# Identity products on TensorE in front of its waits, in a two-block transformer kernel on one core

## The chip, the cores and the metric

The program runs on one core of one Trainium2 chip. The metric is the device time of one execution in microseconds (us). Before the change three executions took 2232.43, 2234.43 and 2234.75 us, median 2234.43.

## What is computed

The reference applies two models of two layers each to 256 tokens of width 1024, in float32, one after the other.

```python
x = first_block(x, ...)     # per layer: mixer_block, layer_norm, then swiglu (layer 0) or moe_ffn (layer 1), layer_norm
return second_block(x, ...) # per layer: modulated rms_norm, attention, modulated rms_norm, gated feed-forward
```

The mixer of the first block projects the tokens with one wide matrix into four branches (windowed attention, an RWKV recurrence, a forgetting attention called fox, and a top-k attention called dsa) and four gates, and joins them. The mixture of experts routes each token to two of eight experts:

```python
logits = (x @ router_w).astype(jnp.float32) + router_b
top_val, top_idx = lax.top_k(logits, TOP_K)
weights = jax.nn.softmax(top_val, axis=-1)
...
y = y + combine[..., e:e + 1].astype(x.dtype) * swiglu(x, w1[e], w3[e], w2[e])
```

The second block adds `g * f(rms_norm(x) * (1 + sc) + sh)` twice per layer, where g, sc and sh are rows made from a conditioning vector.

## The kernel before, in words

Each engine has its own hand-written program; they meet through semaphores. TensorE's program (`pe`, from line 1150) sets the order of the work. The tokens lie as two tiles (t = 0, 1) of 128 rows by 1024 columns; `turn` (line 1172) transposes one tile with eight transposes against the identity matrix `ident`, ScalarE copies the result from PSUM to `xT`, and products against weights follow: `channel_tile` (line 1255) and `token_tile` (line 1262), eight 128-row steps each. Weights come in units of 1 MB (in the experts smaller ones) that SyncE's queue loads into a ring of slots as they come free. One ordinary float32 product call shows as two MATMUL records in the trace, one transpose as one. Independent projections, handed out by `fill`, stand between dependent steps so that TensorE has work while the other engines compute. Where none is left, TensorE waits on a semaphore.

The waits that the change touches, in order of the program:

- **Start** (lines 1696 to 1710): TensorE waits for `ident` from GpSimd, then for the first tokens, and turns them.
- **Mixing** (`tanh`, line 1722): after the projections of the RWKV branch TensorE waits for ScalarE's tanh of the low-rank row (line 855), then makes `w_up`, `a_up` (lines 1725, 1729) and `g_up` (line 1734), in both layers.
- **Attention entry** (line 1875, layer 0): TensorE waits for `pick`, VectorE's scores of the top-k branch (line 2492), before the first attention products (`scores`, line 1522). The fox heads there use products with only four active rows (lines 1526 and 1527).
- **Routing** (lines 1900 to 1911 and `experts`, line 1326): for each tile TensorE turns it and multiplies by the router (line 1904); VectorE finds the two experts (`assigned`); TensorE counts ranks (lines 1330 to 1334); VectorE derives the number of rounds (`rounds`, line 2109) and the gather matrices (line 2127); TensorE loads the number of rounds into a register and gathers the tokens (line 1361).
- **Second block's entry** (`spread`, line 1212): in layer 0 TensorE waits for VectorE's variance of the first tile, then spreads two rows of the modulation over all partitions (line 1220) with four calls of 512 columns. Then the first tile is scaled and turned by products against a diagonal matrix (`turn_scaled`, line 1182), which waits for VectorE's line 2553. In layer 1 `spread(1)` stands after the first two projections, and the third (`project`) waits for VectorE to free its PSUM bank (line 2300).

```python
pe.wait_ge(*ready("dve", "rounds"))
n_rounds = pe.value_load(rounds_i[0:1, 0:1], min_val=1, max_val=3)
...
with S.turns(pe, n_rounds):
    for k in range(KT):
        gather_tokens(0, k)
```

Of the kernel before, what the change touches and what calls it, by code (L numbers as in the profile page):

```python
# [14 lines left out]
P = 128  # L15
# [62 lines left out]
class Signals:  # L78
# [26 lines left out]
    def ready(self, kind, *key, back=0):  # L105
        value, looped = self.known.value[(kind, key)] if self.known else (1, False)
        if looped:
            step = self.known.per_turn[kind]
            return self.sem(kind), self.turn * step + (value + self.credit(kind) - back * step)
        return self.sem(kind), value  # L110
# [19 lines left out]
def build(nc, a, out, known):  # L130
    with ExitStack() as ctx:
# [3 lines left out]
        def sb(name, shape, dt=F32):  # L135
            return ctx.enter_context(nc.sbuf_tensor(name, shape, dt))
# [15 lines left out]
        ident = sb("ident", [P, P])  # L152
# [17 lines left out]
        psum = ctx.enter_context(nc.psum_tensor("psum", [P, 8, 512], F32))  # L170
# [980 lines left out]
        def _(pe):  # L1151
# [3 lines left out]
            def job(ins, *key):  # L1155
                ins.then_inc(*made("pe_job", *key))
# [7 lines left out]
            def used(*key):  # L1164
                S.also("pe_job", "unit", *key)

            def turn(src, tag, t, made_by=None):

                if made_by is not None:
                    pe.wait_ge(*ready("dve", *made_by, t))  # L1170
                for k in range(KT):
                    ins = pe.transpose(psum[:, 2 * t + k // 4, (k % 4) * P:(k % 4) * P + P],
                                       src[:, t, k * P:k * P + P], ident[:])
                job(ins, "xt", *tag, t)
# [11 lines left out]
            def modulated(which, l, t):  # L1186
                pe.wait_ge(*ready("dve", "modulated", which, l, t))
                pe.wait_ge(*ready("act", "modulated", which, l, t))
# [17 lines left out]
            def turn_mod(l, bank):  # L1206

                pe.wait_ge(*ready("mod_turned", l))
                ins = pe.transpose(psum[:, bank, 0:48], mod_turned[0:48, :], ident[0:48, 0:48])
                job(ins, "mod_columns", l)  # L1210

            def spread(l):

                pe.wait_ge(*ready("pool", "g_diag", l))
                if l == 0:
                    pe.wait_ge(*ready("dve", "var", "ln2", 1, 0))
                    pe.wait_ge(*ready("act", "warm", "ln2", 1))
                for i in range(2):
                    for h in range(2):
                        ins = pe.matmul(psum[:, 4 + 2 * i + h, :], ones[:],  # L1220
                                        g_diag[:, i, 4 * h:4 * h + 4].rearrange("p a b -> p (a b)"),
                                        start=True, stop=True)
                    job(ins, "spread", l, i)
# [102 lines left out]
            def experts():  # L1326

                pe.wait_ge(*ready("pool", "numbers"))
                pe.wait_ge(*ready("dve", "assigned"))
                pe.matmul(psum[:, 5, 0:8], before[:], assigned[:, 0, :], start=True, stop=True)  # L1330
                pe.matmul(psum[:, 5, 8:16], ones[:], assigned[:, 0, :], start=True, stop=False)
# [2 lines left out]
                job(pe.matmul(psum[:, 5, 16:24], ones[:], assigned[:, 1, :], start=False, stop=True), "ranks")  # L1334
                pe.wait_ge(*ready("dve", "rounds"))
                n_rounds = pe.value_load(rounds_i[0:1, 0:1], min_val=1, max_val=3)

                def xjob(ins, *key):
                    ins.then_inc(*made("x_pe", *key))
# [345 lines left out]
            for l in range(DEPTH):  # L1685
                if l == 0:
                    pe.wait_ge(*ready("pool", "ident"))
                first = []
                for t in range(NT):
                    if l == 0:  # L1690
# [29 lines left out]
                else:  # L1720
                    turn_mod(0, PAR_BANK)
                fill(l, G[0][l] - 1, (6,))
                pe.wait_ge(*ready("act", "tanh", l))
                for ct in range(2):
                    ins = pe.matmul(psum[:, 0, ct * 256:ct * 256 + 256], lora[0:64, l, 0, ct * P:ct * P + P],
# [44 lines left out]
                for c in range(NC):  # L1770

                    b = (0, 1, 4, 5)[c]
                    for h in range(4):
# [4 lines left out]
                                  start=True, stop=True)  # L1778
# [7 lines left out]
                for lv in range(1, 6):  # L1786
# [11 lines left out]
                    for g in range(2):  # L1798
                        pe.wait_ge(*ready("act", "U", l, lv, g))
                        for m in range(4 * g, 4 * g + 4):  # L1800
                            for odd in range(2):
                                o = (m % 4) * CH
                                pe.matmul(psum[hb(odd), 4 * g + 1, o:o + CH], TT[hb(odd), m, :], U[hb(odd), m, :],
                                          start=True, stop=True)
# [57 lines left out]
                for qt in range(NT):  # L1862
                    nk = P * (qt + 1)
                    for h2 in range(2):
                        for h in range(2):
                            ins = pe.matmul(psum[:, 4 + 2 * qt + h, h2 * 256:h2 * 256 + nk],
                                            dsa_qi[hb(h), h2, qt * P:qt * P + P], dsa_ki[hb(h), 0:nk],
                                            start=True, stop=True)
                    job(ins, "idx", l, qt)
                fill(l, in_attention(l), (0, 1))  # L1870
                for b in (0, 1):
                    if b in fill_in:
                        pe.wait_ge(*ready("act", "filled", l, fill_in[b]))

                pe.wait_ge(*ready("dve", "pick", l, NT - 1))
                attention(l)
                barrier()
# [4 lines left out]
                for c in range(KT):  # L1882
                    if c >= 2:
                        pe.wait_ge(*ready("dve", "prod", l, c - 2))
                    for b in range(4):
                        rows_of = (range(0, 4), range(4, 6), range(6, 8), range(8, 10))[b]
                        dst = psum[:, 4 + 2 * (c % 2) + b // 2, (b % 2) * 256:(b % 2) * 256 + 256]
                        for k in rows_of:
                            ins = pe.matmul(dst, (wb_first[:, k] if k < 5 else wb_last[:, k - 5])[:, c * P:c * P + P], oT[:, k, :],  # L1889
                                            start=(k == rows_of[0]), stop=(k == rows_of[-1]))  # L1890
# [3 lines left out]
                def normalised(t):  # L1894
                    turn(x, ("f1", l), t, ("ln", "ln1", l))
                    pe.wait_ge(*ready("act", "xt", "f1", l, t))

                if l == 0:
                    dense(("ffn1", 0), normalised)
                else:  # L1900
                    for t in range(NT):
                        normalised(t)
                        for k in range(KT):
                            ins = pe.matmul(psum[:, 4, t * 8:t * 8 + 8], xT[:, k, t * P:t * P + P], router[:, k, :],
                                            start=(k == 0), stop=(k == KT - 1))
                    job(ins, "router")
                    pe.wait_ge(*ready("dve", "router_logits"))
                    experts()

            for l in range(DEPTH):  # L1910

                if l == 0:
                    spread(0)
                else:
                    turn_mod(1, 3)
                first = []
                for t in range(NT):
                    turn_scaled("mix", l, t)
                    modulated("mix", l, t)
                    for n in range(2):  # L1920
                        if t == 0:
                            first.append(unit("in2", l, ORDER2[n]))
                        ins = token_tile(psum[:, n, t * 256:t * 256 + 256], first[n], 0, 256, t)
                        if t == 1:
                            job(ins, "in2", l, ORDER2[n])
                            used("in2", l, ORDER2[n])
                if l == 1:
                    spread(1)
                del turned_last[:]
                project(l, 2)  # L1930
                turn_heads(l, 0)
                project(l, 3)
                turn_heads(l, 1)
                project(l, 4)
                turn_heads(l, 3)
                scores2(l, 0)
                project(l, 5)
                turn_heads(l, 4)
                turn_probs2(l, 0)
                scores2(l, 1)  # L1940
                project(l, 6)
                weigh2(l, 0)
                turn_probs2(l, 1)
                scores2(l, 2)
                project(l, 7)
                turn_heads(l, 6)
                turn_outs(l, 0)
                weigh2(l, 1)
                turn_probs2(l, 2)
                scores2(l, 3)  # L1950
                project(l, 8)
                turn_heads(l, 7)
                turn_outs(l, 1)
                weigh2(l, 2)
                turn_probs2(l, 3)
                project(l, 9)
                turn_outs(l, 2)
                weigh2(l, 3)
                scores2(l, 4)
                project(l, 10)  # L1960
                turn_heads(l, 9)
                turn_probs2(l, 4)
                turn_outs(l, 3)
                scores2(l, 5)
                project(l, 11)
                turn_heads(l, 10)
                weigh2(l, 4)
                turn_probs2(l, 5)
                join(l, 0, 0)
                join(l, 0, 1)  # L1970
                scores2(l, 6)
                turn_outs(l, 4)
                weigh2(l, 5)
                join(l, 0, 2)
                join(l, 0, 3)
                scores2(l, 7)
                turn_probs2(l, 6)
                turn_outs(l, 5)
                join(l, 0, 4)
                join(l, 0, 5)  # L1980
                join(l, 1, 0)
                turn_probs2(l, 7)
                weigh2(l, 6)
                join(l, 1, 1)
                join(l, 1, 2)
                turn_outs(l, 6)
                weigh2(l, 7)
                join(l, 1, 3)
                join(l, 0, 6)
                turn_outs(l, 7)  # L1990
                join(l, 1, 4)
                join(l, 0, 7)
                join(l, 1, 5)
                join(l, 1, 6)
                join(l, 1, 7)

                def gated(t):
                    turn_scaled("ffn", l, t)
                    modulated("ffn", l, t)

                dense(("ffn2", l), gated)
# [699 lines left out]
```

## Time and profile before

| | us |
|---|---|
| median of three executions | 2234.43 |
| the profiled execution's own time | 2232.85 |
| its span, first to last instruction | 2231.1 |
| TensorE matmul busy in the span | 2116.5 (95%) |
| VectorE busy | 658.6 (30%) |
| ScalarE busy | 363.8 (16%) |
| mean granted TensorE clock | 0.981 of full |

### The profile page before, as it was taken

How to read it: one execution, taken by the hardware profiler on the slowest of the kernel's cores; microseconds unless marked ns; L12 is line 12 of the kernel's file. 1: busy time of each engine (PE TensorE's matmuls, PEld its weight loads, DVE VectorE, ACT ScalarE, POOL GpSimd, SP SyncE). 2: the span in 40 equal slices, each digit the busy share in tenths (PEclk: the TensorE clock that was granted, in tenths of full speed). 3: DMA queues.
4: the chain of work that ended last, by engine and by line, in shares of the span. 5: the costliest groups of instructions: out<-in, count | busy, mean ns of one | idle time of the engine just before them, and what ended most of it. 6: DMA issues, size and time to landing. Idle time of an engine off the chain costs nothing.

```text
span 2231.1 us, 33975 instructions
## 1 busy us (share of the span) xinstructions
PE 2116.5 (95%) x14688; PEld 1525.7 (68%) x14688; DVE 658.6 (30%) x1635; ACT 363.8 (16%) x861; POOL 83.7 (4%) x180
## 2 busy tenths in 40 slices
PE   8998999999989999998999999899999998999998
PEld 7786776777678877855643553487677757867776
DVE  1415424333334154242010000244433333440001
ACT  1312230000013122300010000133200012430000
POOL 3000000000000000020000000000000020000000
PEclk9999999999999998998999999999999999999999
DMA  8333234688563342337999999942579763224442
GB/s 254 114 96 123 95 123 151 210 274 285 173 193 105 93 139 82 123 97 248 348 313 371 345 323 364 298 133 95 177 232 306 255 183 113 96 95 151 134 149 94
DMA packets 333817, 421.23 MB, mean 189 GB/s; under 512 B 27222, under 2 KB 282148, under 8 KB 333668
## 3 DMA queue, kind: packets, MB, share of 16 engines
q1 hardware_dynamic: 312464, 352.96, 49.1%
q0 software_dynamic: 13408, 50.66, 6.8%
q10 hardware_dynamic: 7796, 15.43, 2.0%
q8 instruction: 116, 1.90, 0.4%
q14 instruction: 33, 0.27, 0.0%
HBM read 417.90 MB, written 1.05 MB: 188 GB/s over the span
## 4 chain that ended last, share of the span: by engine, by line
PE 87%; DVE 4%; ACT 3%; issue 2%; DMA 2%; ACTq 1%; POOL 0%; DVEq 0%; POOLq 0%
PE psum L1255 31%; PE psum L1372 10%; PE psum L1262 9%; PE psum L1273 9%; PE psum L1432 5%; PE psum L1889 3%; PE psum L1502 2%; PE psum L1673 2%; PE psum L1291 2%; PE psum L1361 1%; PE psum L1700 1%; PE psum L1445 1%; DVE arena L2061 1%; ACTq L635 1%; DMA arena<-in_w_mod 1%
## 5 line engine op out<-in xcount | busy, mean ns | idle before, releaser
L1255 PE MATMUL psum<-xT,ring 128*128 128x256 f32 x3520 | 786.4, 384 | 3.9 <-ACT small L758 2.1
L1255 PEld LDWEIGHTS psum<-xT,ring 128*128 128x128 f32 x3520 | 672.5, 192 | 118.9 <-issue 20.5
L1273 PE MATMUL psum<-ring,arena 128*128 128x512 f32 x528 | 232.8, 594 | 0.0
L1262 PE MATMUL psum<-ring,xT 128*128 128x256 f32 (+2 forms) x960 | 205.5, 373 | 11.8 <-DVE arena L2300 4.4
L1262 PEld LDWEIGHTS psum<-ring,xT 128*128 128x128 f32 x960 | 174.4, 194 | 39.9 <-DVE arena L2300 5.7
L1273 PEld LDWEIGHTS psum<-ring,arena 128*128 128x128 f32 x528 | 100.3, 191 | 114.9 <-issue 112.5
L2072 DVE TENSOR_TENSOR arena<-arena,psum 128x512 f32<-128x512 f32 x33 | 22.7, 687 | 407.4 <-PE psum L1255 235.0
L2061 DVE SCALAR_TENSOR_TENSOR arena<-arena,cond 128x256 f32<-128x256 f32 x336 | 135.0, 478 | 0.0
L1372 PE MATMUL psum<-ring,arena 128*32 128x256 f32 x2304 | 126.9, 379 | 0.7 <-DVE arena L2144 0.7
L667 ACT ACTIVATE arena<-psum 128x512 f32<-128x512 f32 x33 | 19.7, 597 | 578.2 <-PE psum L1255 571.9
L1372 PEld LDWEIGHTS psum<-ring,arena 128*32 128x32 f32 x2304 | 74.6, 110 | 51.3 <-issue 3.4
L561 POOL DMA_DIRECT2D arena<-in_w_mod x48 | 42.5, 891 | 1331.7 <-PE psum L1673 605.3
L2152 DVE TENSOR_TENSOR arena<-arena,psum 128x768 f32<-128x768 f32 (+1 forms) x12 | 10.6, 887 | 218.1 <-ACT arena L689 218.1
L1889 PE MATMUL psum<-oT,arena 128*128 128x256 f32 x320 | 69.6, 380 | 4.2 <-DMA arena<-in_w_branch 4.2
L1889 PEld LDWEIGHTS psum<-oT,arena 128*128 128x128 f32 x320 | 60.6, 190 | 13.2 <-DMA arena<-in_w_branch 5.0
L1372 PE MATMUL psum<-arena 128*32 128x256 f32 x1152 | 64.9, 380 | 0.0
L1432 PE MATMUL psum<-ring,arena 128*32 128x512 f32 x576 | 64.2, 594 | 0.0
L1673 PE MATMUL psum<-ring,oT 128*128 128x512 f32 x128 | 56.9, 592 | 0.0
L1502 PE MATMUL psum<-ring,arena 128*128 128x512 f32 x128 | 55.3, 592 | 0.0
L1372 PEld LDWEIGHTS psum<-arena 128*32 128x32 f32 x1152 | 37.0, 110 | 24.6 <-issue 1.0
L1291 PE MATMUL psum<-xT,ring 128*128 128x128 f32 x384 | 44.4, 276 | 9.3 <-ACT xT L968 7.0
L744 ACT ACTIVATE arena<-psum,par 128x256 f32<-128x256 f32 x64 | 26.9, 471 | 161.1 <-PE psum L1255 161.1
(392 smaller groups left out, 1865.5 us busy)
## 6 DMA issues: line engine op xcount, KB each, us to landing
ring<-in_w_in SPq DMA_DIRECT2D x80, 1024.0 KB, 5.4
ring<-in_exp_w SPq DMA_DIRECT2D x312, 256.0 KB, 6.0
arena<-in_w_mod POOLq DMA_DIRECT2D x48, 1024.0 KB, 10.1
ring<-in_ffn_w SPq DMA_DIRECT2D x33, 1024.0 KB, 6.1
arena<-in_exp_w SPq DMA_DIRECT2D x120, 256.0 KB, 6.8
ring<-in_w_gate SPq DMA_DIRECT2D x22, 1024.0 KB, 7.7
ring<-in_w_up SPq DMA_DIRECT2D x22, 1024.0 KB, 10.1
ring<-in_w_down SPq DMA_DIRECT2D x22, 1024.0 KB, 5.1
```

Of the source, the lines that this page charges most:

```text
L561: pool.dma_start(modw[:, j % 3, :].rearrange("p (k c) -> p k c", k=KT), w_mod[:, :, j * UNIT:(j + 1) * UNIT]).then_inc(*made("modw%d" % (j ...
L744: step(act.activation(zb[:, b, c, :], bank[:, i * 256:i * 256 + 256], ACT.Identity, bias=prm(l, "gate_b", b * KT + c)), "filled", l, j)
L1255: ins = pe.matmul(dst, w[:, k * 256 + c0:k * 256 + c0 + m], act_t[:, k, :], start=(k == 0), stop=(k == KT - 1))
L1262: ins = pe.matmul(dst, act_t[:, k, t * P:t * P + P], w[:, k * 256 + c0:k * 256 + c0 + n], start=(k == 0), stop=(k == KT - 1))
L1273: ins = pe.matmul(psum[:, 4 + 2 * t + h, :], gT[:, s % 3, f * 256 + t * P:f * 256 + t * P + P], w2[:, f * D + h * 512:f * D + h * 512 + 51 ...
L1291: ins = pe.matmul(psum[:, i, f * 256 + t * P:f * 256 + t * P + P], wt[i][:, k * 256 + f * P:k * 256 + f * P + P], xT[:, k, t * P:t * P + P ...
L1372: ins = pe.matmul(psum[GRP * (g % 4):GRP * (g % 4) + GRP, o[0] + g // 4, o[1]:o[1] + n], xgT[:, k, GRP * g:GRP * g + GRP], slot[:, w0:w0 + n],
L1432: ins = pe.matmul(psum[GRP * (g % 4):GRP * (g % 4) + GRP, 3 * d + g // 4, :], hT[:, j, GRP * g:GRP * g + GRP], slot[:, w0:w0 + 512], start ...
L1502: ins = pe.matmul(psum[:, 2 * t + h, :], mergedT[:, k, t * P:t * P + P], ws[k2][:, i * D + h * 512:i * D + h * 512 + 512], start=(k == 0), ...
L1673: ins = pe.matmul(psum[:, 4 * t + h, :], oT8[:, k, t * P:t * P + P], w[:, (k % 2) * D + h * 512:(k % 2) * D + h * 512 + 512], start=(k == ...
L1889: ins = pe.matmul(dst, (wb_first[:, k] if k < 5 else wb_last[:, k - 5])[:, c * P:c * P + P], oT[:, k, :], start=(k == rows_of[0]), stop=(k ...
L2061: free(dve.scalar_tensor_tensor(out=pmod[:, i, :], in0=w, scalar=cond[:, k:k + 1], in1=pmod[:, i, :], op0=ALU.mult, op1=ALU.add), "mod", l, i)
```

## The change

A helper `keep_clock(bank, n)` issues n products of the identity matrix with itself, 128 by 128 each, into a PSUM bank that nothing reads at that point. It is called nine times, 81 products in all, 162 MATMUL records. No other instruction is added, removed or moved on any engine. In TensorE's program each call stands behind whatever it had to wait for before that place, and ahead of the wait named here.

| place | products | ahead of the wait for |
|---|---|---|
| start | 6 | first tokens |
| mixing, layer 0 | 4 | tanh |
| mixing, layer 1 | 10 | tanh |
| attention entry, layer 0 | 10 | pick (behind the wait for the last projection's copy) |
| routing, between the tiles | 5 | second tile normalised |
| routing, after the logits | 8 | assigned |
| routing, after the register load | 18 | gather matrices |
| second block, layer 0 | 6 | variance of the first tile |
| second block, layer 1, after spread(1) | 14 | bank of the third projection |

```diff
+            def keep_clock(bank, n):
+
+                for _ in range(n):
+                    pe.matmul(psum[:, bank, 0:P], ident[:], ident[:], start=True, stop=True)
...
                 pe.wait_ge(*ready("pool", "g_diag", l))
                 if l == 0:
+                    keep_clock(3, 6)
                     pe.wait_ge(*ready("dve", "var", "ln2", 1, 0))
...
                 pe.wait_ge(*ready("pool", "numbers"))
+                keep_clock(0, 8)
                 pe.wait_ge(*ready("dve", "assigned"))
...
                 n_rounds = pe.value_load(rounds_i[0:1, 0:1], min_val=1, max_val=3)
+                keep_clock(0, 18)
...
                 if l == 0:
                     pe.wait_ge(*ready("pool", "ident"))
+                    keep_clock(7, 6)
...
                 fill(l, G[0][l] - 1, (6,))
+                keep_clock(7, (4, 10)[l])
                 pe.wait_ge(*ready("act", "tanh", l))
...
+                if l == 0:
+                    keep_clock(3, 10)
                 pe.wait_ge(*ready("dve", "pick", l, NT - 1))
                 attention(l)
...
                     for t in range(NT):
+                        if t == 1:
+                            keep_clock(7, 5)
                         normalised(t)
...
                 if l == 1:
                     spread(1)
+                    keep_clock(3, 14)
```

## Rows read from the trace of the kernel before

**Rows 1.** The page: busy time, granted clock in 40 slices, and the chain.

```profile
PE 2116.5 (95%) x14688; PEld 1525.7 (68%) x14688; DVE 658.6 (30%) x1635; ACT 363.8 (16%) x861; POOL 83.7 (4%) x180
...
PEclk9999999999999998998999999999999999999999
...
PE 87%; DVE 4%; ACT 3%; issue 2%; DMA 2%; ACTq 1%; POOL 0%; DVEq 0%; POOLq 0%
```

**Rows 2.** Stretches: length, busy of PE, PEld, DVE, ACT, POOL, granted clock, DMA.

```profile
202.80:206.20 3.40, 0.52 (x7) 0.55 (x8) 3.15 (x8) 1.27 (x1) 0.00 (x0) 1.00 0.96 295
206.20:209.60 3.40, 3.40 (x11) 2.25 (x9) 2.67 (x7) 0.00 (x0) 0.00 (x0) 0.50 0.09 27
243.70:247.10 3.40, 3.40 (x17) 2.07 (x15) 0.00 (x0) 0.00 (x0) 0.00 (x0) 1.00 0.31 106
247.10:250.60 3.50, 3.50 (x9) 2.83 (x9) 3.19 (x8) 1.03 (x5) 0.00 (x0) 0.51 0.00 0
1015.20:1022.00 6.80, 6.19 (x10) 3.46 (x11) 1.11 (x2) 0.48 (x1) 0.00 (x0) 0.50 1.02 340
1022.00:1028.80 6.80, 6.80 (x22) 4.02 (x22) 1.11 (x2) 1.44 (x3) 0.00 (x0) 1.00 1.07 341
```

**Rows 3.** Timeline, one of the fox products in the first of the stretches at 243.7.

```profile
246.04 0.69 PE L1526 MATMUL psum<-arena,ident 4*128 4x256 f32 x2
```

**Rows 4.** Timeline, attention entry: start, us, engine, line, idle before and releaser.

```profile
205.68 1.22 PE L1522 MATMUL psum<-arena 64*128 64x128 f32 x8 [3.78 <-DVE arena L2492]
```

**Rows 5.** Timeline, mixing in layer 0 (first two) and layer 1.

```profile
65.49 0.48 PE L1725 MATMUL psum<-arena,lora 64*128 64x256 f32 x1 [0.99 <-ACT arena L855]
...
68.18 2.11 PE L1255 MATMUL psum<-xT,ring 128*128 128x256 f32 x9
...
670.32 0.74 PE L1725 MATMUL psum<-arena,lora 64*128 64x256 f32 x1 [3.79 <-ACT arena L855]
...
673.99 2.32 PE L1255 MATMUL psum<-xT,ring 128*128 128x256 f32 x10
```

**Rows 6.** Timeline, routing.

```profile
992.53 1.95 PE L1904 MATMUL psum<-router,xT 128*128 128x8 f32 x16 [1.16 <-ACT xT L658]
996.87 1.97 PE L1172 MATMUL psum<-ident,x 128*128 128x128 f32 x8 [2.39 <-DVE x L2038]
1000.00 3.58 PE L1904 MATMUL psum<-router,xT 128*128 128x8 f32 x16 [1.16 <-ACT xT L658]
...
1006.71 0.56 PE L1330 MATMUL psum<-arena 128*128 128x8 f32 x2 [3.13 <-DVE arena L2100]
...
1011.46 0.88 SPq L465 DMA_DIRECT2D oT<-in_exp_w  x2
...
1015.81 13.63 PE L1361 MATMUL psum<-arena,x 128*128 128x384 f32 x32 [6.83 <-DVE arena L2127]
```

**Rows 7.** Timeline, entry of the second block, layer 0.

```profile
1427.42 5.37 PE L1220 MATMUL psum<-arena,ones 128*128 128x512 f32 x8 [2.58 <-issue]
...
1432.43 0.29 DVE L2553 TENSOR_SCALAR arena<-ident,small 128x128 f32<-128x128 f32 x1
...
1432.77 2.05 PE L1182 MATMUL psum<-arena,x 128*128 128x128 f32 x16
```

**Rows 8.** Timeline, second block, layer 1.

```profile
1843.93 7.14 PE L1262 MATMUL psum<-ring,xT 128*128 128x256 f32 x32 [1.75 <-DVE arena L2583]
...
1850.91 3.60 PE L1220 MATMUL psum<-arena,ones 128*128 128x512 f32 x8
...
1858.92 10.20 PE L1262 MATMUL psum<-ring,xT 128*128 128x256 f32 x32 [4.41 <-DVE arena L2300]
```

**Rows 9.** Timeline, start of the program.

```profile
1.24 0.29 POOL L511 TENSOR_SCALAR_AFFINE_SELECT ident<-ident 128x128 f32<-128x128 f32 x1 [0.24 <-POOL ident L510]
...
4.81 1.94 PE L1172 MATMUL psum<-ident,x 128*128 128x128 f32 x8 [4.81 <-POOL tri L507]
7.91 9.17 PE L1700 MATMUL psum<-xT,ring 128*128 128x128 f32 x64 [1.16 <-ACT xT L658]
```

## The prediction

> **What bounds the kernel now.** I read the page first. TensorE is busy for 95% of the span and holds 87% of the chain that ended last [rows 1]. The reader should see two consequences: a microsecond less on TensorE is nearly a microsecond less of time, and products added between its waits cost nothing only as long as they end before the wait does. Then the clock row: all 9s but for two 8s [rows 1]; the mean is 0.981. Cutting the span into stretches shows where the halves lie. At the attention entry TensorE is nearly idle from 202.8 to 206.2, at clock 1.00; then it is busy throughout from 206.2 to 209.6, at 0.50 [rows 2]. The clock falls behind the idle time, and it is the work after the wait that pays. The same pattern stands behind the waits for tanh in layer 1, for the second tile in routing, for the gather, and at both entries of the second block. The idle times ahead of the fallen clock are 3.78 us at the attention entry [rows 4], 3.79 for tanh in layer 1 [rows 5], 2.39 and then 6.83 in routing [rows 6], 2.58 in the second block's layer 0 [rows 7] and 4.41 in layer 1 [rows 8]. The 0.99 us in front of tanh in layer 0 brought no fall [rows 5].
>
> Not every fall follows idleness: from 243.7 to 247.1 TensorE is busy throughout, with fox products of four rows among its work, and the clock is halved from 247.1 [rows 2, 3]. The change leaves those places alone.
>
> **What an added product costs.** A call gives two records of 128 columns. At full clock 16 ordinary records of that shape take 2.05 us [rows 7], and 16 of the router 1.95 [rows 6]: 0.12 to 0.13 us each, I take 0.12. At half clock the router's 16 take 3.58 [rows 6] and eight transposes 1.97: 0.22 to 0.25, I take 0.23. A call is thus 0.24 us warm and 0.46 cold.
>
> For bf16 the Trainium skill (TensorE: Matmul & The Clock Gate, "Wait — 56ns, not 53.3ns?") has 56 ns for 128 columns warm and 107 cold; by its figures all fillers below would cost half and none would overrun its wait, which would add the 2.5 us of overrun below to the gain. The float32 rows here show twice those figures, and the sum goes by the rows.
>
> **Place by place.**
>
> *Start.* `ident` is there at 1.53, the first product starts at 4.81 [rows 9]: 3.3 us, into which 12 cold records (2.8 us) fit. The row of granted clock is not recorded here, but the durations tell: eight transposes take 1.94 us where 0.12 each would be 1.0 [rows 9]. The next 64 records take 9.17 us; at 0.12 they would take 7.7. So at most 0.9 + 1.5 = 2.4 us is to be had, if the clock rises before 4.8; at the least nothing. I take the middle, 1.2.
>
> *Mixing, layer 0.* Eight records, 1.0 us, in 0.99 us of idle time [rows 5]. The clock stays up anyway: 0, at worst 0.1 lost. *Layer 1.* Twenty records, 2.4 us, in 3.79: 1.4 us of idleness are left. From L1725 to the projection behind it takes 2.69 us in layer 0 (65.49 to 68.18) and 3.67 in layer 1 at half clock (670.32 to 673.99) [rows 5]: **1.0**.
>
> *Attention entry.* Behind the copy that it waits for (about 202.8) 20 records end at 205.2, ahead of 205.68 [rows 4]. The stretch 206.2 to 209.6 is then at full clock: half of 3.4 is 1.7 [rows 2], less a little for waits, **1.6**. TensorE has projections queued behind, so this stays.
>
> *Routing.* Gains: ten of the 32 gather records run cold, 6.19 us where at full clock 22 take 6.80 (0.31 each): +3.2 [rows 2]. The second tile's router products 3.58 against 1.95: +1.6, of which I count half, since those eight-column products do little to hold a clock that the five calls before them raised [rows 6]. Costs: the eight calls start near 1003.9, when the logits are read. Cold they take 3.7 us, to 1007.6, and the rank counts behind them started at 1006.71 [rows 6]: 0.9 late cold, nothing warm; I take 0.5. The eighteen calls start once the register is loaded; SyncE, which loads the same number, issues at 1011.46 [rows 6], so 4.3 us are left to 1015.81. Thirty-six records take 4.3 us warm and 8.3 cold: 0 to 4.0 late. Half and half they are 2.0 late, which I take, since TensorE has been idle or nearly so for long before them and starts them cold. Sum 3.2 + 0.8 - 0.5 - 2.0 = **1.5**. The bounds are +5.6 (3.2 + 1.6 and 0.8 for the cold rank counts) and -4.9.
>
> *Second block, layer 0.* Twelve records, 1.4 us, fit in 2.58. The spread products would take 3.60 [rows 8] instead of 5.37 [rows 7], 1.8 less, but the next product starts at 1432.77, right behind VectorE's diagonal matrix, ready at 1432.72 [rows 7]. That becomes the wait: **0**. The dip behind 1438.4 follows other waits and stays.
>
> *Second block, layer 1.* Twenty-eight records, 3.4 us, in 4.41. The 32 projection records take 10.20 us instead of 7.14 [rows 8]: up to 3.0. This half clock lasts twice as long as the others; with one of the usual length it would be 1.6. I take the mean, **2.3**.
>
> **Sum:** 1.2 + 1.0 + 1.6 + 1.5 + 0 + 2.3 = 7.6 us, with bounds of the terms from about +13 to -1. Against the profiled 2232.85 that is 2225.3; against the median, which is 1.58 higher, **2226.8 us**. What also moves: all later work starts earlier, and the falls after fox products will land otherwise; about 2 us either way.
>
> **The rivals.**
>
> *The clock falls just the same (slower).* If multiplying the identity does not count as work for the clock, the gains are nil and the fillers still stand in the way: in routing 0.9 + 4.0 us at half clock, elsewhere they fit. 2234.4 + 4.9 = 2239.3. For it speaks that busy TensorE with four-row products did not hold the clock [rows 2, 3]; against it, that the filler has 128 active rows like the products that do. It decides if the stretch behind the attention entry and that behind spread(1) still read 0.50. The Trainium skill (TensorE: Matmul & The Clock Gate, "Part 4: PE-mode transpose") has that transposes do not count as busy for the clock in the same way. By that rule, were it to reach identity products, this rival would be the outcome; here the filler is an ordinary product, and no row shows identity products alone. Chance 0.08.
>
> *Held, but eaten (same).* The clock is held, but routing overruns fully while its gather still gains (3.2 - 4.9 = -1.7), the start gives nothing, and layer 1's spread gives 1.6: 1.0 + 1.6 - 1.7 + 1.6 = 2.5 us, 2231.9; or VectorE becomes the wait behind mixing and attention and takes 1 to 2 us back. For it: VectorE's 3.15 of 3.40 us at the attention entry [rows 2]. Chance 0.22.
>
> *The forecast,* 2222 to 2230, with its centre at 2226.8. Chance 0.70.
>
> **How the numbers follow.** A measurement of this kernel can tell about 0.2%, 4.5 us, from no change: faster means under 2230.0, slower over 2238.9. So faster 0.70, same 0.22, slower 0.08. The range runs from 2222 (start and routing both near their best) to 2233, which takes in the second rival and leaves out the first and the extremes.
>
> **What would show it.** In the changed profile the stretches behind tanh in layer 1, behind the attention entry, behind spread in layer 0 and behind spread(1) read 1.00; the 32 records after spread(1) take about 7.1 us; L1725 to the next projection 2.7; the gather's 32 records near 10.5 instead of 13.6. The gather starts later after the rank counts than the 9.1 us of before (1006.71 to 1015.81) if I am right on the overrun. The mean clock rises from 0.981 to about 0.99. A gather that starts on VectorE's release, with no filler ahead of it, would show the routing cost too high, and half clock behind any of the four fillers would show the mechanism wrong there.

## The result, and the profile after

| | before | changed |
|---|---|---|
| median, us | 2239.20 | 2227.93 |
| lowest to highest | 2230.62 to 2245.74 | 2218.88 to 2232.29 |
| executions | 16 | 16 |
| profiled execution, us | 2232.85 | 2223.20 |
| mean granted clock in it | 0.981 | 0.986 |

The ratio is 0.995, with a 95% interval from 0.9936 to 0.9963: 11.2 us faster, between 8.3 and 14.3. The median before is 4.8 us above that of the three executions shown first, which lie in the lower half of its range. So the predicted time, 2226.8, is met within 1.1 us and its range (2222 to 2233) holds it, but the predicted gain of 7.6 us is below the measured interval. Two errors of the forecast met: it started too low and took off too little.

The page of the changed kernel answers to [rows 1]:

```profile
PE 2127.5 (96%) x14850; PEld 1542.0 (69%) x14850; DVE 658.9 (30%) x1635; ACT 363.3 (16%) x861; POOL 83.3 (4%) x180
...
PEclk9999899999999999989999999999999999999999
```

TensorE has 162 records more and is busy for 11.0 us more in a span that is 9.6 us shorter. Four of the nine calls stand here, in the timeline of the changed kernel (start, us, engine, line, operation, count, idle before and releaser); line 1170 is the filler:

```profile
203.07 2.50 PE L1170 MATMUL psum<-ident 128*128 128x128 f32 x20 [0.93 <-ACT arena L744]
205.83 0.93 PE L1530 MATMUL psum<-arena 64*128 64x128 f32 x8 [0.26 <-DVE arena L2507]
...
664.27 2.44 PE L1170 MATMUL psum<-ident 128*128 128x128 f32 x20
668.21 0.48 PE L1735 MATMUL psum<-arena,lora 64*128 64x256 f32 x1 [1.50 <-ACT arena L855]
...
1416.48 1.50 PE L1170 MATMUL psum<-ident 128*128 128x128 f32 x12
1419.17 3.70 PE L1226 MATMUL psum<-arena,ones 128*128 128x512 f32 x8 [1.19 <-DVE small L2045]
1424.57 2.05 PE L1187 MATMUL psum<-arena,x 128*128 128x128 f32 x16 [1.70 <-DVE arena L2568]
...
1847.72 3.29 PE L1170 MATMUL psum<-ident 128*128 128x128 f32 x28
1852.30 7.17 PE L1268 MATMUL psum<-ring,xT 128*128 128x256 f32 x32 [1.29 <-DVE arena L2315]
```

Each filler ends before its wait does, since the work behind it is still released by ScalarE or VectorE. The attention products take 0.93 us for 1.22 [rows 4], the spread 3.70 for 5.37 [rows 7] and the projection behind `spread(1)` 7.17 for 10.20 [rows 8]. In the second block's layer 0 the diagonal matrix is now waited for (1.70 us, line 2568), which gives the spread's gain away.

Stretches of the changed kernel (columns as in [rows 2]); the first two answer to those at the attention entry there, the others lie behind tanh in layer 1, behind the spread in layer 0, behind `spread(1)` and at fox in layer 0:

```profile
203.00:206.40 3.40, 3.07 (x28) 2.84 (x28) 3.15 (x8) 1.30 (x2) 0.00 (x0) 1.00 0.90 278
206.40:209.80 3.40, 3.40 (x18) 2.77 (x15) 3.00 (x8) 0.14 (x1) 0.00 (x0) 1.00 0.14 46
...
671.60:675.00 3.40, 3.40 (x17) 3.00 (x16) 3.23 (x6) 0.22 (x1) 0.00 (x0) 1.00 0.00 0
...
1419.20:1422.60 3.40, 3.40 (x8) 1.41 (x8) 2.88 (x4) 0.44 (x2) 0.00 (x0) 1.00 0.01 3
...
1852.20:1859.20 7.00, 6.90 (x32) 6.11 (x33) 4.04 (x20) 0.51 (x2) 0.00 (x0) 1.00 0.00 0
...
244.40:251.20 6.80, 6.80 (x16) 4.87 (x16) 3.93 (x9) 1.86 (x8) 0.00 (x0) 0.50 0.00 0
```

The clock behind these four waits is full. Behind the fox products it falls as before, in this execution for twice as long (6.80 us for 3.50 [rows 2]).

Routing is where the calls get in the way (timeline of the changed kernel):

```profile
989.37 1.97 PE L1177 MATMUL psum<-ident,x 128*128 128x128 f32 x8 [1.17 <-DVE x L2053]
992.50 3.58 PE L1918 MATMUL psum<-router,xT 128*128 128x8 f32 x16 [1.16 <-ACT xT L658]
996.42 3.78 PE L1170 MATMUL psum<-ident 128*128 128x128 f32 x16 [0.34 <-DVE small L2540]
999.99 0.43 PE L1337 MATMUL psum<-arena 128*128 128x8 f32 x2
...
1004.50 6.41 PE L1170 MATMUL psum<-ident 128*128 128x128 f32 x36 [2.37 <-DVE arena L2129]
1010.75 10.49 PE L1369 MATMUL psum<-arena,x 128*128 128x384 f32 x32
```

The turn (1.97) and the router products (3.58) of the second tile are still at half clock. The eight calls run cold (0.24 us a record) straight into the rank counts, and the eighteen start cold and run straight into the gather: TensorE shows no wait behind either, so both overrun. The gather itself takes 10.49 us for the old 13.63 [rows 6].

To compare places across traces I take, for each, the time between the starts of two of the old products around it. "Without" is the mean over traces whose kernel has no working filler there, "with" over the others; e1's four-row filler counts as none everywhere but in routing, where it is left out, as are the two runs with smaller calls there. The last two places have no filler near them; "with" means there that the kernel has fillers ahead of the place, e1 among them.

| place | without | with | gain | predicted |
|---|---|---|---|---|
| start (second turn's start) | 17.09 | 16.25 | 0.8 (ranges overlap) | 1.2 |
| tanh, layer 0 | 4.06 | 4.06 | 0 | 0 |
| attention entry | 13.8 | 12.05 | 1.7 | 1.6 |
| tanh, layer 1 | 7.79 | 6.75 | 1.0 | 1.0 |
| `y_sq`, layer 1 (line 1862) | 9.37 | 7.68 | 1.7 | not named |
| routing, turn to end of gather | 39.2 | 39.1 | 0.1 | 1.5 |
| spread(0) to turn | 8.52 | 8.52 | 0 | 0 |
| spread(1) to the turned heads | 14.3 | 12.02 | 2.3 | 2.3 |
| wait for the branch weights, layer 0 (line 1901) | 2.9 | 2.2 | 0.7 | not named |
| wait for the modulation (line 1207) | 3.4 | 1.9 | 1.5 | not named |

For `y_sq` the classes are "fell" and "didn't fall" (see e9 to e12). At the start the traces with a filler run from 15.46 to 18.07 and those without from 16.51 to 17.89, so that its 0.8 is not shown. The places down to `spread(1)` sum to 7.6 us, all of them to 9.8.

The last two gains don't come from the clock. Some 600 us into the program TensorE waits for VectorE, and VectorE for a transfer of modulation weights. Timelines of before, of the changed kernel and of e1, whose fillers have four rows:

```profile
599.98 1.91 PE L1202 MATMUL psum<-arena,ones 128*1 128x256 f32 x32 [2.99 <-DVE arena L2061]
```

```profile
597.88 1.91 PE L1207 MATMUL psum<-arena,ones 128*1 128x256 f32 x32 [1.33 <-DVE arena L2076]
```

```profile
603.94 1.91 PE L1207 MATMUL psum<-arena,ones 128*1 128x256 f32 x32 [1.29 <-DVE arena L2076]
```

The products take 1.91 us in all three; only the wait differs. VectorE waited 10.48 us for its transfer in before, 8.83 in the changed kernel and 8.79 in e1. From product to product this place takes 3.2 to 3.6 us in the five traces of kernels with no filler ahead of it (before, e5, e8, e9, e11) and 1.9 to 2.0 in the other nine. The wait for the branch weights, near 315 us, divides the traces in the same way (2.8 to 3.1 us against 2.1 to 2.5). Why the transfers land earlier relative to TensorE when the kernel has more products ahead of them, or in all, is open.

### The profile page after: what moved, and what is told of

The parts are those of the page before. It is cut to its first block, busy times and chain, and to the rows that moved or that the text cites. A ratio compares the mean times of both kernels' runs of the same rounds, so it can differ in the third digit from the quotient of the medians.

```text
span 2221.5 us, 34297 instructions
## 1 busy us (share of the span) xinstructions
PE 2127.5 (96%) x14850; PEld 1542.0 (69%) x14850; DVE 658.9 (30%) x1635; ACT 363.3 (16%) x861; POOL 83.3 (4%) x180
## 4 chain that ended last, share of the span: by engine, by line
PE 87%; DVE 4%; ACT 3%; DMA 3%; issue 2%; ACTq 1%; POOL 0%; SPq 0%; DVEq 0%; POOLq 0%
PE psum L1261 31%; PE psum L1380 10%; PE psum L1268 9%; PE psum L1279 9%; PE psum L1440 5%; PE psum L1901 3%; PE psum L1510 2%; PE psum L1681 2%; PE psum L1297 2%; PE psum L1369 1%; PE psum L1453 1%; ACTq L635 1%; DVE arena L2076 1%; PE psum L1709 1%; DMA arena<-in_w_branch 1%
## 5 line engine op out<-in xcount | busy, mean ns | idle before, releaser
L1901 PEld LDWEIGHTS psum<-oT,arena 128*128 128x128 f32 x320 | 60.6, 190 | 13.1 <-DMA arena<-in_w_branch 4.9
```

## The experiments

The theory: TensorE's clock falls after a stretch in which it does little, and an identity product of 128 rows counts as work. The main rival has the gain come from something else that more products bring, or has any product count. The two waits for transfers above show that something else is at work too, for some 2 of the 11 us. Edits are against the changed kernel unless said otherwise. Ratios are to the kernel before, with 95% intervals. The first four kernels shared one set of runs of the kernel before (median 2237.04, 27 executions), e5 to e8 another (2240.54, 23 executions).

### e1: the same fillers with four rows

```diff
-                    pe.matmul(psum[:, bank, 0:P], ident[:], ident[:], start=True, stop=True)
+                    pe.matmul(psum[:, bank, 0:P], ident[0:4, :], ident[0:4, :], start=True, stop=True)
```

> The changed kernel with all 81 fillers kept, but each multiplies only four rows of the identity (ident[0:4, :] by itself) instead of 128. My theory (the clock falls when few rows of TensorE have been at work for a while, whether TensorE counts as busy or not): a filler of four rows takes as long as one of 128 and holds nothing, so the work behind the attention entry, behind tanh in layer 1 and behind spread(1) runs at half clock again (32 records after spread(1) in 9 to 10.5 us instead of 7.1), and the fillers of routing run wholly cold. Time near 2239 + 3 to 5 = 2242 to 2244. Rival (any instruction in flight on TensorE holds the clock, however many rows): the same as the changed kernel, 2228, with 7.1 us behind spread(1).

Measured: 2239.01 us (2233.22 to 2245.14, 12 executions), ratio 1.0007 (0.9989 to 1.0025), clock 0.977. The attention entry, timeline and then stretches, of this run:

```profile
205.80 2.49 PE L1170 MATMUL psum<-ident 4*128 4x128 f32 x20 [0.93 <-ACT arena L744]
208.56 0.93 PE L1530 MATMUL psum<-arena 64*128 64x128 f32 x8 [0.27 <-DVE arena L2507]
```

```profile
206.60:210.00 3.40, 3.13 (x27) 2.56 (x26) 3.03 (x7) 0.45 (x1) 0.00 (x0) 1.00 0.87 291
210.10:213.50 3.40, 3.40 (x10) 2.69 (x9) 3.09 (x11) 1.11 (x5) 0.00 (x0) 0.50 0.01 2
```

Twenty records take 2.49 us, as with 128 rows, and TensorE is busy for 3.13 of 3.40 us; yet the next stretch is at 0.50. The same number of products of the same duration doesn't hold the clock, so the time that the engine is busy doesn't decide it. The two kernels differ in the rows that take part, 4 or 128, and with them in the number of ones that go through the array, also 4 or 128; these two were not told apart. All the fallen places are back (attention entry 13.74 us, tanh 7.7, `y_sq` 9.37, spread(1) 14.83), and routing, where the fillers now only delay, is at 43.79 us, 4.6 above the 39.2 without any. The expectation had 2242 to 2244, that is these delays on top of before; the two shorter waits for transfers, 2.2 us, which e1 shares with the changed kernel, take it most of the way down to 2239.01.

### e2: fox products with 128 rows, in the changed kernel

```diff
-                    four = slice(HD * h, HD * h + 4)
-                    head = ident[four, HD * h + hd:HD * h + hd + 1]
+                    head = ident[:, HD * h + hd:HD * h + hd + 1]
...
-                            pe.matmul(dst, head.broadcast_to([4, P]), fox_t[four, 1, 0:nk], start=False, stop=False)
-                            ins = pe.matmul(dst, fox_t[four, 0, qt * P:qt * P + P], head.broadcast_to([4, nk]),
+                            pe.matmul(dst, head.broadcast_to([P, P]), fox_t[:, 1, 0:nk], start=False, stop=False)
+                            ins = pe.matmul(dst, fox_t[:, 0, qt * P:qt * P + P], head.broadcast_to([P, nk]),
```

The identity's column is zero outside its one row, so the rows added to the sum are multiplied by zero. Only eight rows of `fox_t` are written; the others hold what earlier work left in that part of the arena, so the edit is sound only as long as these leftovers are finite numbers.

> The changed kernel with the fox products of four rows made products of 128 rows: the one-hot column has 127 zeros, so the sum is the same, and no record takes longer. If the number of active rows is what the clock goes by, the falls within attention (three in the trace before, three in the trace after, some 17 us at half clock in the changed one) are gone: 5 to 9 us less than the changed kernel, 2219 to 2223, and the mean clock rises from about 0.984 to about 0.991. Rival (the falls there come from short gaps between the small products, not from the rows): no difference from the changed kernel, 2228, with half clock behind the fox products as before.

Measured: 2211.49 us (2208.75 to 2214.82, 6 executions), ratio 0.988 (0.9853 to 0.9907), clock 0.991. One of its fox products, and two stretches behind such, in fox of layer 0 and of layer 1:

```profile
247.26 0.70 PE L1533 MATMUL psum<-arena,ident 128*128 128x256 f32 x2
```

```profile
248.40:251.80 3.40, 3.40 (x17) 2.99 (x17) 3.16 (x8) 1.00 (x5) 0.00 (x0) 1.00 0.00 0
...
856.00:870.00 14.00, 14.00 (x76) 11.17 (x75) 3.77 (x8) 3.39 (x11) 0.00 (x0) 1.00 0.24 76
```

With 128 rows the product takes 0.70 us, with four it took 0.69 [rows 3]. The fox part of layer 0 takes 25.79 us, against 31.1 to 34.4 in the eleven traces with four-row products, and that of layer 1 24.52, against 29.8 to 33.1. So it was the four-row products that those stretches fell behind, although TensorE was busy throughout. The gain over the changed kernel, some 16 us, is about twice the 5 to 9 expected: the two fox parts alone are 5.3 to 8.6 us shorter each.

### e3 and e4: routing without fillers, and with fewer

```diff
-                keep_clock(0, 8)
...
-                keep_clock(0, 18)
...
-                        if t == 1:
-                            keep_clock(7, 5)
```

> The changed kernel without the three fillers in routing (5, 8 and 18 calls), all others kept. Theory: routing is a net gain of 0 to 2 us only, since the fillers there start cold and overrun their waits by 0.8 and 1.8 us in the one trace and give 3.1 us back in the gather. So 2228 to 2230, the gather's 32 records 13 to 13.6 us again, and its start 7.2 us after the last rank count instead of 9.0. Rival (routing, with its longest stretch at half clock, carries much of the gain): 2233 or more.

```diff
-                keep_clock(0, 8)
+                keep_clock(0, 6)
...
-                keep_clock(0, 18)
+                keep_clock(0, 10)
```

> The changed kernel with 6 instead of 8 calls ahead of assigned and 10 instead of 18 behind the register load, so that they fit their waits even at half clock (12 records by 0.213 in 2.8 us, 20 in 4.5). Theory: what follows is work of the same weight, so nothing is lost by stopping when the wait is over: rank counts 3.5 us after the last router product, gather 7.2 after the last rank count instead of 9.0, and the gather's clock rises about when it did. 1 to 2.5 us less than the changed kernel: 2225.5 to 2227. Rival (the clock needs the longer run of fillers to have risen by the gather): the gather takes 13 us again and the time is 2228 or more.

Measured: e3 2229.23 us (2222.99 to 2238.48, 12 executions), ratio 0.997 (0.9948 to 0.9992); e4 2227.04 us (2220.43 to 2230.57, 10 executions), ratio 0.9944 (0.9924 to 0.9965). Both times are as expected (2228 to 2230, and 2225.5 to 2227), but the two intervals and that of the changed kernel overlap, so the totals can't rank them. The place can: routing takes 38.60 us in e3 and 36.95 in e4. The timeline of e4:

```profile
1003.08 2.93 PE L1170 MATMUL psum<-ident 128*128 128x128 f32 x12 [0.34 <-DVE small L2540]
1005.80 0.57 PE L1337 MATMUL psum<-arena 128*128 128x8 f32 x2
...
1010.45 4.63 PE L1170 MATMUL psum<-ident 128*128 128x128 f32 x20 [2.37 <-DVE arena L2129]
1014.92 10.78 PE L1369 MATMUL psum<-arena,x 128*128 128x384 f32 x32
```

Twelve cold records take 2.93 us for the sixteen's 3.78, and twenty 4.63 for the thirty-six's 6.41. From the last router product to the rank counts it is 3.42 us (4.27 with eight calls, 3.49 with none), and from the last rank count to the gather 7.20 us (8.7 to 9.1 with eighteen calls, 7.19 with none): both overruns are gone, and the gather is still warm but for one or two of its 32 records.

### e5: fox products with 128 rows, and no fillers at all

The edit of e2, made in the kernel before:

```diff
-                    four = slice(HD * h, HD * h + 4)
-                    head = ident[four, HD * h + hd:HD * h + hd + 1]
+                    head = ident[:, HD * h + hd:HD * h + hd + 1]
```

> The kernel before, without any filler, with the fox products made 128 rows wide as in the second experiment. Theory (rows at work hold the clock; the two edits mend different places): its gain over the kernel before is that of the second experiment over the changed kernel, about 16 us, so 2220 to 2224 where before is 2237, with no half clock inside the stretch from the first fox product to the end of attention, and the falls behind the other waits as before. Rival (the two help only together, for instance because the fillers shift the fox products): under half of it, 2230 or more.

Measured: 2221.11 us (2220.44 to 2223.57, 6 executions), ratio 0.9929 (0.9906 to 0.9953), some 16 us. Its median gain is above the 11.2 us of all the fillers, with intervals that overlap, and it adds no product. Its fox parts take 25.79 and 24.52 us as in e2; its attention entry (13.78), tanh (7.7) and `y_sq` (9.37) are as slow as before. The two gains add up: 0.9929 times 0.995 is 0.988, what e2 measured.

### e6: what the runs so far suggest, together

The edits of e2 and e4, and two more fillers:

```diff
+                keep_clock(3, 7)
                 pe.wait_ge(*ready("dve", "y_sq", l))
...
                     turn_scaled("mix", l, t)
+                    if t == 0:
+                        keep_clock(2, 8)
                     modulated("mix", l, t)
```

> All together: 128-row fox products, the fillers of the change with 6 and 10 calls in routing instead of 8 and 18, and two more places: 7 calls ahead of the wait for y_sq at the end of the recurrence in both layers, 8 calls between the scaled turn of the first tile and the wait for its copies in both layers of the second block. Theory: 2 us less from routing, 1 us each for two falls that a trace shows behind those waits in some executions: 2207 to 2210 against 2211.5 of the second experiment. Rival (the added fillers run over their waits as in routing, or delay the copies): 2211 or more.

Measured: 2207.80 us (2206.38 to 2209.12, 5 executions), ratio 0.9867 (0.9841 to 0.9894), clock 0.991. It beats both kernels; over e2, whose interval it shares, it is not shown to be better. Its page, and the timeline at the second block's entry:

```profile
PE 2118.4 (96%) x14890; PEld 1538.7 (70%) x14890; DVE 658.8 (30%) x1635; ACT 363.3 (16%) x861; POOL 83.7 (4%) x180
...
PEclk9999999999999999989999999999999999999999
```

```profile
1411.36 1.95 PE L1170 MATMUL psum<-ident 128*128 128x128 f32 x16
1413.71 7.17 PE L1268 MATMUL psum<-ring,xT 128*128 128x256 f32 x32 [0.40 <-DVE xT L2577]
```

This projection took 8.86 us in the profiled changed kernel, behind a 2.19 us wait. From the first turn to the third projection it is 22.10 us here and 23.79 in most traces; in e4 and e7 it was 22.1 without a filler, so that this one's worth is not shown, and neither is that of the one at `y_sq`, where e2 didn't fall without it. The one 8 left in the clock row is routing.

### e7: without the start, tanh layer 0 and spread(0)

```diff
-                    keep_clock(3, 6)
...
-                    keep_clock(7, 6)
...
-                keep_clock(7, (4, 10)[l])
+                keep_clock(7, (0, 10)[l])
```

> The changed kernel without the fillers at the start, ahead of tanh in layer 0 and ahead of spread(0). By my working tanh and spread(0) are worth nothing and the start about 1 us: 2228 to 2230 where the changed kernel has 2228. Rival (each filler carries its share, 24 of 81... here 16 of 81 calls): 2230 to 2232.

Measured: 2231.94 us (2226.06 to 2234.93, 12 executions), ratio 0.9966 (0.9951 to 0.9982). That is above the 2228 to 2230 expected and nearer to the rival (2230 to 2232), but the interval overlaps that of the changed kernel, so whether the three matter is not shown. The places say that two of them don't (4.06 and 8.52 us, as in every trace), and that the second turn starts at 17.31, within what both kinds of kernel show there.

### e8: the routing fillers alone

Against the kernel before:

```diff
+                keep_clock(0, 8)
...
+                keep_clock(0, 18)
...
+                        if t == 1:
+                            keep_clock(7, 5)
```

> The kernel before with the three fillers of routing alone (5, 8 and 18 calls). Theory: worth 0 to 2 us, so 2235 to 2238 where before is 2237; the gather starts 8.5 to 10 us after the last rank count instead of 7.2, and its 32 records take 10.3 to 11 us. Rival (most of the gain is here): 2232 or less.

Measured: 2241.32 us (2222.53 to 2245.49, 12 executions), ratio 0.9995 (0.9971 to 1.0018). Nothing measurable (2235 to 2238 was expected), as the place has it: its gather takes 10.49 us for 13.63, and it starts 9.09 us after the last rank count instead of 7.19.

### e9 to e12: does the filler ahead of tanh spare `y_sq` its fall?

In layer 1, TensorE waits 1.59 us for `y_sq` between two products. Timeline of before and of the changed kernel:

```profile
789.49 1.74 PE L1852 MATMUL psum<-arena,block_ones 128*128 128x512 f32 x2 [1.59 <-DVE arena L2460]
```

```profile
786.42 1.12 PE L1862 MATMUL psum<-arena,block_ones 128*128 128x512 f32 x2 [1.59 <-DVE arena L2475]
```

The wait is the same, no filler stands near it, and yet the clock fell in one and not in the other. It fell in before, e1, e5 and e8, which have no working filler ahead of tanh, and in none of the five that did then (after, e2, e3, e4, e7; e6 has a filler of its own here). The theory was that the fall at tanh, 120 us earlier, brings this one about. Two kernels, each run twice: e9 and e11 are the kernel before with only the ten calls ahead of tanh in layer 1; e10 and e12 the changed kernel without them.

```diff
                 fill(l, G[0][l] - 1, (6,))
+                keep_clock(7, (0, 10)[l])
```

```diff
-                keep_clock(7, (4, 10)[l])
+                keep_clock(7, (4, 0)[l])
```

> The kernel before with one filler alone, the ten calls ahead of tanh in layer 1. The traces so far have the clock fall behind the wait for y_sq, 120 us later in the same layer, in all four kernels without a working filler at tanh (the kernel before, the first, fifth and eighth experiments), and in none of the five with it and without a filler at y_sq. Theory of a knock-on (where the clock last fell and rose sets whether it falls at y_sq; the missing fall at tanh moves that): no fall at y_sq here, from the product for the mean to the seventh projection product behind it 7.7 us instead of 9.4. Rival (chance, or the fillers of layer 0): it falls, 9.4 us. Of the whole only 1 to 3 us.

> The changed kernel without the ten calls ahead of tanh in layer 1. Theory of a knock-on: the clock falls at tanh (7.7 instead of 6.75 us to the projection behind it) and again at y_sq (9.4 instead of 7.7 us). Rival (chance, or the other fillers): 7.7 us at tanh, 7.7 at y_sq.

> The ninth experiment's kernel once more, since one trace is one draw of where the clock's steps lie: the theory has 7.7 us at y_sq in both traces, the rival a mix.

> The tenth experiment's kernel once more: the theory has 9.4 us at y_sq in both traces, the rival a mix.

Measured, one execution each: e9 2242.62 and e11 2237.57 us, e10 2239.23 and e12 2228.46, beside 2237.33 for the kernel before; single executions that differ by up to 11 us for one kernel say nothing of its total. The place: with the filler alone, `y_sq` doesn't fall (7.67 us, twice). Without the filler and with all others it doesn't fall either (7.67, twice), though tanh does. Half of the theory holds and half doesn't. Timeline of e12:

```profile
668.94 0.79 PE L1735 MATMUL psum<-arena,lora 64*128 64x256 f32 x1 [3.78 <-ACT arena L855]
...
672.82 3.49 PE L1261 MATMUL psum<-xT,ring 128*128 128x256 f32 x15
```

In e10 and e12 the fall at tanh lasts 6.8 us, where it lasted 3.4 in the four traces that fell at `y_sq`. What decides between them is open: of the thirteen traces without a filler at this place the two falls come together in four, tanh's alone in two, none in seven. With the same wait of 1.59 us the clock fell in four traces and stayed in nine.

## Why the prediction was right, and where it was not

**The mechanism holds.** The four stretches named read 1.00; the 32 records behind `spread(1)` took 7.17 us (7.1 said), and tanh's line to the projection 2.70 (668.21 to 670.91; 2.7 said). The gather took 10.49 (10.5 said) and starts 10.76 us after the rank counts begin (999.99 to 1010.75; 9.1 before), later as the overrun implied. The clock rose to 0.986, not quite the 0.99 given.

**Attention entry, mixing, both spreads** were priced at 1.6, 0, 1.0, 0 and 2.3 us and measured 1.7, 0, 1.0, 0 and 2.3. The three gains were read from what the same work took at the other clock, and the one zero with a saving in it (spread in layer 0) from what was ready next, VectorE's diagonal matrix, and that wait is in the profile now.

**Start** was sized at the middle of 0 to 2.4 us, and the means differ by 0.8 with ranges that overlap. The upper bound left out the weights: in the changed kernel's trace the products behind the first turn wait for a transfer twice (1.53 us, then 0.41 until 11.79), and the second turn starts at 15.46, 1.5 us earlier than before, although the 64 products ahead of it ran at full clock.

**Routing was the term mis-sized:** +1.5 was said, 0.1 measured. Its step "of which I count half" (+0.8 for the second tile's router products) failed: with five calls ahead of the wait those products took 3.58 us in the changed kernel as before. The overruns were close (0.5 and 2.0 said, 0.8 and 1.5 to 1.9 measured against none). And the +3.2 of the gather (its row gives 3.1: ten records at 0.31 less) was read from one trace near its worst: without fillers the gather takes 13.1 to 14.4 us to the next product, so that against 11.2 warm it gains 1.9 to 3.2. The two overruns eat that. e4 shows that it was to be had: 2.3 us, with calls counted at half clock. The prediction said that they start cold and still priced them half and half.

**What it missed:** the fall at `y_sq` (1.7 us), an idle time that was in the trace and was not looked at, since the change puts nothing there; and the two shorter waits for transfers (2.2 us), which no clock explains.

**The sum.** The places that were priced give 5.9 us where 7.6 was said; those that weren't, `y_sq` and the two transfers, add 3.9, if the kernel before falls at `y_sq` in every execution as it did in its one trace. Together that is 9.8 where 11.2 (8.3 to 14.3) was measured. That the predicted time was met within 1.1 us is therefore luck in part: a start 4.8 us too low stood against a gain 3.6 us too small. The granted clock gives a second account, an estimate: its mean over the 16 executions of the changed kernel is 0.984, over the 50 of the kernel before beside e1 to e8 it is 0.978, and the unrounded difference of 0.0057 over some 2235 us is 13 us given back at most, before the overruns in routing are taken off. The falls behind fox and at other short waits land differently from one execution to the next (fox in layer 1 took 29.8 us in the profiled changed kernel and 33.0 to 33.1 in most others), and one trace of a kernel doesn't tell their mean. One of them speaks against a gain: a part of the second block's attention in layer 0 took 29.9 us before, in e1, e7 and e11, and 31.6 in the profiled changed kernel and in all others. "About 2 us either way" was said of them; whether their mean moved with the change is open, and it could be the 1.4 us that the places lack.

**The rivals.** "The clock falls just the same" is out for 128 rows, and e1, with the four-row filler, is what it describes: routing lost 4.6 us there for the 4.9 said. That its 2239.3 is near e1's 2239.01 is luck, since the kernel before was at 2237.04 beside e1 and not at 2234.4, and the shorter waits for transfers made up for it. The rule of the Trainium skill (TensorE: Matmul & The Clock Gate, "Part 4: PE-mode transpose") that transposes don't count as busy in the same way does not reach ordinary products of the identity with itself, mostly zeros as they are: the trace after them reads 1.00. "Held, but eaten" had routing right in direction (-1.7 said, 0.1 measured) and the rest wrong.

## What to carry to other kernels

Where the clock row shows halves, list what TensorE did just before each fall: idleness is one cause, and products of few rows are another that a busy share hides. Widen the few-row products with zeros first, since it cost no time here (some 16 us gained, and no product added), and see to it that the rows they are multiplied with hold finite numbers; then put fillers into waits, as many as fit at half clock and no more. Price a filler by its cold duration wherever TensorE was idle before it, and look for the next thing that will be waited for: a saving ahead of it is nothing. Compare waits for transfers too before a gain is put down to the clock.

## What the hardware showed that was not expected

- Records of four rows took what records of 128 rows take (2.49 and 2.50 us for twenty; 0.69 and 0.70 for a fox pair), but a stretch full of them left the next at half clock. Where between 4 and 128 rows it changes was not tried.
- Products that are mostly zeros held the clock: the fillers have 127 zeros to a one in each row, and e2's wide fox products are zeros on one side but for one row. Products of nothing but zeros were not tried.
- The same program shows different falls in different executions: the fox part of layer 0 took 34.3 us in e9 and 31.1 in e11, which are one kernel. With wide products it took 25.79 in all three traces.
- Transfers far from any filler moved with the change: a wait of 2.99 us became 1.33, and 1.29 with four-row fillers, at the same granted clock of 1.00.
- The kernels without four-row products also scatter less: e2, e5 and e6 lie within 6.1, 3.1 and 2.7 us, in five or six executions each, the others within 9 to 23 in ten or more.
